# Convolution taps of the values moved one tile at a time into the levels of the delta rule, and the keys' transposes one step later

## The reference

```python
proj = h @ w_in                                  # dn_qkv is its first 1536 columns
qkv = jax.nn.silu(causal_depthwise_conv(dn_qkv, dn_conv))   # 4 taps per channel
q, k, v = jnp.split(qkv, [512, 1024], axis=-1)   # 4 heads of 128 each
q = l2_normalize(q); k = l2_normalize(k)
beta = sigmoid(dn_b); g = -exp(A_log) * softplus(dn_a + dt_bias)
# chunks of 64: G = cumsum(g); decay = exp(G_i - G_j); m = strict(beta k k^T * decay)
sol = triangular_solve(m + I, [v * beta, k * beta * exp(G)])    # -> u, w
# then a scan over the chunks with the state S
```

## Time and profile before

| | |
|---|---|
| median of 3 runs | 1890.44 us (1889.96 to 1891.81) |
| the profiled execution | 1886.58 us, span 1884.8 us, mean granted clock 0.998 |
| TensorE, PE / PEld | 1852.0 us (98%) / 1767.1 us (94%) |
| VectorE | 1251.8 us (66%) |
| ScalarE | 956.6 us (51%) |
| GpSimd | 307.5 us (16%) |

### The profile page before, as it was taken

How to read it: one execution, slowest core, us unless ns; L and a number is a source line. 1 busy time by engine, 2 the same in 40 slices (tenths; PEclk the granted TensorE clock), 3 DMA queues, 4 the chain that set the end, 5 groups by cost and what they waited for, 6 DMA issues and landing times.

```text
span 1884.8 us, 36462 instructions
## 1 busy us (share of the span) xinstructions
PE 1852.0 (98%) x15492; PEld 1767.1 (94%) x15492; DVE 1251.8 (66%) x1676; ACT 956.6 (51%) x1381; POOL 307.5 (16%) x176
## 2 busy tenths in 40 slices
PE   7999999999999999999999999999999999999998
PEld 7889998998888999999989999999999999999998
DVE  6884677665679547777648765576547694567743
ACT  5634466444564345654545455555535445556633
POOL 0050221000002203200001442320001352321000
PEclk9999999999999999999999999999999999999999
DMA  6453354655445334655666553356555663455663
GB/s 237 152 162 113 124 164 162 204 191 190 154 148 169 123 103 137 199 182 183 196 202 192 185 170 123 124 190 196 187 188 177 213 201 113 135 170 188 191 201 102
DMA packets 92161, 317.59 MB, mean 169 GB/s; under 512 B 11744, under 2 KB 12896, under 8 KB 91744
## 3 DMA queue, kind: packets, MB, share of 16 engines
q1 hardware_dynamic: 91424, 314.69, 51.1%
q10 hardware_dynamic: 576, 0.57, 0.1%
HBM read 305.00 MB, written 1.05 MB: 162 GB/s over the span
## 4 chain that ended last, share of the span: by engine, by line
PE 83%; DVE 11%; ACT 3%; issue 1%; DMA 1%; SPq 0%; DVEq 0%; ACTq 0%
PE bank L2007 82%; DVE wlo L1131 4%; DVE area L1131 3%; DVE area L1137 2%; ACT area L634 1%; ACT whi L640 1%; PE bank L2564 1%; DVE hl L1137 1%; DVE xT L1137 1%; DMA raw<-in_weights 1%; SPq L576 0%; DVE area L1651 0%; DVE area L1649 0%; ACT L622 0%; PE bank L2582 0%
## 5 line engine op out<-in xcount | busy, mean ns | idle before, releaser
L1131 DVE TENSOR_TENSOR wlo<-raw,whi 128x1024 fp32r<-128x1024 f32 x518 | 660.7, 1291 | 405.2 <-ACT whi L640 404.8
L2007 PE MATMUL bank<-hh,whi 128*128 128x256 f32 x2928 | 831.3, 285 | 18.4 <-DVE wlo L1131 16.3
L2007 PE MATMUL bank<-hh,wlo 128*128 128x256 f32 x2928 | 816.1, 280 | 0.0
L2007 PE MATMUL bank<-hl,whi 128*128 128x256 f32 x2928 | 809.1, 280 | 0.0
L640 ACT CAST whi<-raw 128x1024 fp32r<-128x1024 f32 x572 | 589.5, 1046 | 400.1 <-PE bank L2007 354.9
L2007 PEld LDWEIGHTS bank<-hh,whi 128*128 128x128 f32 x2928 | 553.2, 189 | 32.5 <-DVE wlo L1131 19.1
L2007 PEld LDWEIGHTS bank<-hl,whi 128*128 128x128 f32 x2928 | 552.4, 190 | 1.4 <-issue 1.4
L2007 PEld LDWEIGHTS bank<-hh,wlo 128*128 128x128 f32 x2928 | 553.2, 189 | 0.0
L1787 POOL TENSOR_TENSOR area<-area 128x512 f32<-128x512 f32 (+4 forms) x86 | 135.5, 1583 | 570.2 <-DVE area L1137 252.9
L1787 POOL TENSOR_TENSOR wlo<-raw,whi 128x1024 fp32r<-128x1024 f32 x54 | 133.7, 2478 | 397.5 <-ACT whi L640 397.5
L2007 PE MATMUL bank<-FH,whi 128*128 128x256 f32 x640 | 179.2, 280 | 0.0
(11 more groups left out here) (132 smaller groups left out, 1904.5 us busy)
## 6 DMA issues: line engine op xcount, KB each, us to landing
raw<-in_weights SPq DMA_DIRECT2D x572, 512.0 KB, 4.0
area<-area SPq DMA_DIRECT2D x96, 64.0 KB, 3.8
area<-area SPq DMA_DIRECT2D x16, 128.0 KB, 3.9
cst<-in_const SPq DMA_DIRECT2D x1, 1188.0 KB, 8.2
cst<-in_const SPq DMA_DIRECT2D x1, 1024.5 KB, 5.7
xT<-in_x SPq DMA_DIRECT2D x4, 256.0 KB, 7.7
out<-xT SPq DMA_DIRECT2D x4, 256.0 KB, 2.9
area<-in_lev SPq DMA_DIRECT2D x2, 384.0 KB, 7.1
```

Of the source, the lines that this page charges most:

```text
L1131: return v.tensor_tensor(dst, x, y, op)
L2007: return e.matmul(ps, x, y, start=start, stop=stop, skip_group_check=skip)
```

## The change

No arithmetic changes. (1) `conv` on VectorE runs the taps two tiles later: those of tiles m0-6 and m0-5 in place of m0-4 and m0-3. The last four tiles, 8 to 11, no longer stand ahead of the delta rule: they are added singly (`tap`), tile 8 at level 1, 9 and 10 at level 2, 11 at level 3. (2) `silu` on ScalarE moves with them: two tile pairs less by the end of `qkv`, `silu(4)` and `silu(6)` ahead of and behind chunk 12's step, `silu(8)` at level 2, `silu(10)` at level 3. (3) At level 1 TensorE transposes the keys after the first chunk of `fill` instead of before it, and VectorE writes `KT` behind that chunk's pass.

```diff
@@ scalar: delta(L, silu) @@
                     yield 1
+
+                    if s in (2, 3):
+                        silu(2 * s + 4)
                     yield 1
@@ scalar: conv in first(L) @@
-                    if m0 > 4:
-                        silu(m0 - 6)
+                    if m0 > 6:
+                        silu(m0 - 8)
@@
+                silu(4)
                 next(fill)
                 silu(6)
                 next(fill)
-                silu(8)
                 next(fill)
-                silu(10)
@@ vector: delta(L, tap) @@
                         tt(quarter(pair(T0, j)), quarter(bank[j]), wide(lev(s), 1, 4), OP.mult).then_inc(*v_dn.up("T0", L, s, j))
+
+                    if s < 4:
+                        tap((8, 9, 11)[s - 1])
+                    yield 1
                     if s == 1:
                         v.wait_ge(*a_dn.at("kx", L))
                         for j in range(2):
                             v.wait_ge(*e_dn.at("KT", L, j))
                             tt(quarter(pair(KT, j)), quarter(bank[2 + j]), wide(kx[:, 4 * j:4 * j + 4], 2, 128), OP.mult).then_inc(*v_dn.up("KT", L, j))
-                    yield 1
...
                         tt(pair(t, j), pair(t, j), bank[b + j][:, :], OP.subtract).then_inc(*v_dn.up("X", L, s, j))
+                    if s == 2:
+                        tap(10)
@@ vector: conv in first(L) @@
-                    if m0 > 2:
-                        taps(m0 - 4)
+                    if m0 > 4:
+                        taps(m0 - 6)
+
+                def tap(m):
+
+                    v.wait_ge(*a_dn.at("tap", L, m))
+                    for j in range(1, 4):
+                        x = stt(A3[:, m, j:T], U3[:, m, 0:T - j], cw[:, m, 3 - j:4 - j], A3[:, m, j:T], OP.mult, OP.add)
+                        if j < 3:
+                            x.then_inc(*v_dn.up())
+                            v.wait_ge(*v_dn.now())
+                    x.then_inc(*v_dn.up("conv", L, m))
@@
                 next(fill)
-                taps(8)
+                taps(6)
                 next(fill)
-                taps(10)
                 next(fill)
@@ tensor: delta(L) @@
                     if s > 1:
                         fresh2(2, lambda j: a_dn.at("Y", L, s, j))
                         sub_turned(("XT", L, s), X, 2)
-                    else:
+                    yield 1
+                    if s == 1:
                         fresh2(2, lambda j: v_dn.at("KB", L, j))
                         turned(e_dn, ("KT", L), Ak, 2)
-                    yield 1
                     e.wait_ge(*v_dn.at("T0", L, s, 1))
```

More of the change, by code:

```diff
@@ L710, in post_finish, with delta @@
                     square(then, j)
-            def delta(L):
+            def delta(L, silu):
                 act(hs(be), AB[:, 0:4, :], AF.Exp, scale=-1.0).then_inc(*a_dn.up("eb", L))
@@ L896, in first @@
                 a.wait_ge(*v_dn.at("ab", L))
-                dn = delta(L)
+                dn = delta(L, silu)
                 next(dn)
@@ L1216, in post_finish, with delta @@
                     low(then, j)
-            def delta(L):
+            def delta(L, tap):
                 tt(hs(a_), AB[:, 4:8, :], hs(Q("dtb", L)), OP.add).then_inc(*v_dn.up())
@@ L1431, in conv @@
                     scaled("qkv", L, U)(m0)
-                    if m0 > 2:
-                        taps(m0 - 4)
-                def taps(m0):
[L1437 to L1444, removed]
+                    if m0 > 4:
[8 more added lines that the diff above has]
+                    x.then_inc(*v_dn.up("conv", L, m))
+                def taps(m0):
+                    tap(m0)
+                    tap(m0 + 1)
                 def hook():
@@ L1461, in first @@
                 v.wait_ge(*v_dn.now())
-                dn = delta(L)
+                dn = delta(L, tap)
                 next(dn)
```

## The result

The changed kernel takes 1909.47 us (median of 4 runs, 1907.48 to 1910.86), the kernel before on the same chip 1890.75 (4 runs, 1889.96 to 1891.81): ratio 1.0091, 95% interval 1.0079 to 1.0103. It is 18.7 us slower, where I had forecast 1.9, and the time lies above my range. The profiled execution took 1910.86, with a span of 1909.1.

The account below looks back on a forecast made before the run. TensorE, busy 98% of the span, was taken as the bound, with about 10 us of waits to win; two layers at +0.95 us gave +1.9 us, 1890.44 to 1892.3 us, range 1887.0 to 1896.2.

Parts of the forecast that it names:

- The front: Up to the sums: no wait at chunk 11, 0.9 at 13, 2.6 at 15, 1.1 at the sums; TensorE 1.5 us behind.
- To level 1: From sums to level 1: the 1.6 us wait at the keys' transposes gone, XLX waiting 0.2 instead of 0.7.
- At levels 2 and 3 taps 9, 10 and 11 are covered: Levels 2 and 3: these taps cost no wait; X of level 2 done 1 us ahead of TensorE's chunk.
- only the COPY does it: Level 1: only GpSimd's COPY, not its TENSOR_TENSOR, stretches VectorE's pass, which took 2.19 instead of 1.22.
- The lower bound of a layer (0): Levels: the pass escapes GpSimd's COPY, VectorE is 0.97 earlier, and a layer costs 0 of 0 to 1.9 us.
- that sum (1.25): LX of level 2: TensorE waits 1.25 us for X, behind T0, tap 8, pass 31 and KT on VectorE.
- Stretched taps: Rival, levels: GpSimd stretches each tap to 2.6 instead of 1.43; a layer +2.1 to +3.1, median 1895 to 1896.5; chance 0.12.
- the pass's factor of 1.8: Levels, stretched-taps rival: each tap takes the pass's 1.8-fold, so tap 8 adds 1.15 us ahead of X.
- The falling clock: Rival: the 2.6 us wait drops TensorE to half clock, 2 x 1.7 us more, 1895.7; chance 0.08.

Follow-up runs that it names:

- silu_later: The changed kernel with silu(4) one step later, behind the cast of chunk 15 instead of ahead of it: 1900.33 us, ratio 1.0061 to the kernel before.
- split_taps: The changed kernel with each instruction of taps 8 to 11 cut into two halves, same computation: 1913.28 us, ratio 1.0122 to the kernel before.
- late_pool: The changed kernel with GpSimd's means and rotations held until tap 11 is done: 1891.72 us, ratio 1.0007 to the kernel before.
- the mended kernel: The changed kernel with GpSimd's means held until tap 11 and silu(4) behind cast 15: 1887.55 us, ratio 0.9984; again 1885.95 us, 0.9979.
- small_pool: The changed kernel with GpSimd's work beside the levels shrunk, pooling and rotations not computed: 1890.74 us, ratio 0.9990 to the kernel before.
- no_taps: The changed kernel without VectorE's taps of tiles 8 to 11, that convolution part left out: 1891.38 us, ratio 1.0002 to the kernel before.
- its two variants: The mended kernel with the keys' transposes back at the first step (1886.61 us, 0.9983), or with tap 8 behind X and KB (1886.38 us, 0.9986).

## Why the prediction was wrong

**The front was right, in size too.** No wait at chunk 11; 1.10, 2.57 and, in layer 1, 1.2 at the sums stand where I had 0.9, 2.6 and 1.1. In layer 0 the half clock from 63.15 on takes the place of the wait at the sums, since TensorE itself is late. The reason given, cast 15 behind silu(4) behind tap 5, is shown by `silu_later`.

**To level 1 it was right.** No wait at the transposes, 0.23 at XLX. AT at 109.36 stood 0.7 ahead of LX at 110.09, as forecast, both 1.2 later than I had them.

**The step that failed** is the price of a tap in the levels: a tile of taps at 1.43, and "At levels 2 and 3 taps 9, 10 and 11 are covered". It rested on "only the COPY does it", my reading of one row: the pass at 107.68 took 1.22 beside the product of 107.94. That pass had begun before the product, so it held its turn. The product was the one that paid: it took 3.18, where GpSimd's product of 1020 columns takes 1.89 in the changed kernel (113.75). The pass at 110.01, which took 2.19, came second, and waited for the product's end at 111.1: 1.1 us, about what it was too long (2.19 against 1.22). The row that I took as evidence against the rival was the winner's side of the same rule. The lower bound of a layer (0), for which the pass had to escape the COPY, fell with it: the pass took 2.22. Tap 8 cost 3.60, tap 9 5.53, the passes behind them 1.62 and 2.29. With GpSimd out of the way taps take 1.50, and the first wait is 0.84, so the rest of that sum (1.25) would have stood. `split_taps` shows at tap 8 that the loss goes with the instructions, `late_pool` that all of it hangs on GpSimd's place in time.

**The rivals.** Stretched taps (0.12) happened, at 2.1 and 4.0 us a tap instead of the 1.2 that I had taken from the pass's factor of 1.8. A factor was the wrong form: a row of one instruction gives a loss of up to one GpSimd instruction, and a tap has three. The Trainium skill, "SBUF — State Buffer", section "SBUF: two separate sides", states the rule in this form, an exclusive lock for the whole of an instruction, first come first served. The traces agree with it: 2.21 with no COPY near, 5.80 for six instructions. I had weighed only the contention of which the Trainium skill speaks in "GPSIMD Engine Reference", section "Key points". The falling clock (0.08) happened too, and came on top: I had both as separate cases, but here most long waits brought the clock down, so one carries the other. By the estimate above the clock makes some 6.2 us.

**What stays open.** When a long wait brings the clock down: those of 3.35 at level 2 of layer 0 and of 2.48 at chunk 15 of layer 1 had no fall, those of 3.35 at level 2 of layer 1 and of 2.57 at chunk 15 of layer 0 had one. Why the same products take 3 to 4% longer in some stretches, which differ from run to run. And whether the mended kernel beats the one before.

## What to carry to other kernels

Before a chain of dependent two-input VectorE instructions is moved, look at GpSimd's timeline at the new place: each link can cost up to a whole GpSimd instruction, so the price goes by links and by the other engine's instructions, as long as it has any, and not by a factor on the busy time. If the chain must go there, let GpSimd start after it, where its results are needed late. On an engine that feeds another through casts, put what can wait behind the cast, not ahead of it. And when two rivals are both "a long wait", ask whether one brings the other.

## What the runs showed of the hardware

- In these traces VectorE instructions with two SBUF inputs and GpSimd's take turns, whole instructions at a time, and both sides pay: a pass 2.2 instead of 1.22, a COPY 2.04 instead of 1.04. VectorE's instructions with one input in PSUM kept their length beside GpSimd (the evacuation and T0 at 112.70: 2.47 for four, beside GpSimd's COPY and product of 111.64 to 115.64; in `late_pool`, at 111.29, with GpSimd standing still, 2.47 too).
- Cut in two, a tap instruction costs 0.25 more undisturbed ((2.27 - 1.51) / 3) and 0.73 more beside GpSimd ((5.80 - 3.60) / 3).
- TensorE's clock fell to 1.2 GHz (granted 0.50) with 22 of the 27 waits of 2 us and more that lie behind the start of the span in the fourteen traces, in part before the wait was over, and once behind one of 1.88 (`split_taps`, 135.43). Five had no fall: 3.35 (122.78) and 2.48 in the changed kernel, 2.55 and 2.45 in `small_pool`, 2.46 in `late_pool`. In `no_taps` a wait of 2.46 at that same place of layer 1 had one. So no length of wait decides it here.
- One fall in the kernel before, 669.8, and one near 176 to 181 in each of five experiments had no such wait ahead of them. The mended kernel and its two variants, whose longest wait behind the start is 1.2 us, had one of that kind or none; the last 3 to 5 us of the span are at the lower level in every run. Each stretch was 3.4 us, or 6.8 for two together.
- At a granted clock of 1.00 the same products ran at two paces: one of 128x256 started 113 ns behind the last, or 118 ns, for up to 170 us at a time, and not in the same stretches in every run. In 140 us near the end, with TensorE busy throughout at a granted clock of 1.00, the kernel before did 1237 products (1720 to 1860) and the changed one 1191 (1740 to 1880). Some of the spread of single runs comes from this, whatever the kernel.
